# Output layers of three attentions as three products of rounded parts, and the second block's norms moved behind the products

## The chip, the core and the metric

The kernel runs on one core of one Trainium2 chip. The metric is device time in microseconds (us), the median of three runs. The profiler's record of one execution gives the rows below.

## The reference, cut to what matters

Two blocks follow each other on x, 512 tokens by 1024 features, all in fp32. The first has two layers; each is FFN, mixer, FFN, and the mixers are a pair of attentions (FoX and a top-k "DSA") in layer 0 and MLA in layer 1:

```
h = h + 0.5*g1*swiglu(rms(h)*(1+sc1)+sh1)
h = h + g2*mixer(rms(h)*(1+sc2)+sh2)      # mixer ends in: mixed @ w_out
h = h + 0.5*g3*swiglu(rms(h)*(1+sc3)+sh3)
h = rmsnorm(h, final_g)                   # end of the first block
```

The second block has two layers more: `u = rmsnorm(h, norm1)`, an input layer for three mixers (mLSTM, differential attention, HGRN), `h += mixed @ w_out`, then `h += relu(rmsnorm(h, norm2) @ w_up)**2 @ w_down`. A norm divides each token (a column of h) by the root of its mean square.

## The kernel before, in words

Features lie on the partitions: h, u are 8 chunks of 128 features by 512 tokens. A dense layer goes slab by slab: a slab holds the weights for 256 outputs (2048 columns; for a down layer 128 outputs), SP loads it into one of four slots of `ring`, and waits for `lin_done` of the slab four before. `ORDER` lists all layers; its last field says whether a layer is *cut*.

In a cut layer weights and inputs are each split into a rounded part (fp32r) and a remainder, and each pair of 128x128 weights and 128x512 inputs is three products: high x high, remainder x high, high x remainder. ScalarE writes a slab's rounded part (`high(q)`, into one of two halves of `w_hi`, after `lin_done` of cut slab q-2), GpSimd the remainder in place in the ring (`rest(q)`, then `w_cut`). Both run two slabs ahead (`layer`). The uncut layers multiply whole fp32. These are `mlaq`, `mlak`, `mlav` and the output layers `hybo`, `mlao`, `wo0`, `wo1`; the last four have 4 slabs of 16 pairs each.

A norm before a layer: ScalarE squares each chunk when it is final (`hrms`), GpSimd adds the squares up (`squares`), PE sums over partitions (`total_sum`), ScalarE takes the root, VectorE the reciprocal, PE spreads it over the partitions (`spread`), VectorE scales each chunk into u (`scale_in`), ScalarE rounds it (`high_input`), VectorE takes the remainder. In `linear`, slab 0 of such a layer takes its products in the order in which chunks arrive (`Fresh`). With `cut_at` (4, 6) the first two slabs of the next layer are rounded ahead of chunks 4 and 6 of the squares, with (7,) one ahead of chunk 7 and the other after.

The attentions go in steps of one head (or two) and 128 queries: PE scores, VectorE maximum, ScalarE exp, VectorE scaling of E (L1828, L1874), PE transposes, ScalarE copy, PE values. ScalarE and VectorE each work through one fixed order, written out by hand. After the last head, `hybo` or `mlao` reads u. In the second block the mLSTM's 16 steps stand between the differential attention and `wo`; `out_products` does chunks 2 to 7 of `wo` slabs 0 and 1 while the mLSTM's own norm (chunks 0, 1) is under way.

## Time and profile before

| | |
|---|---|
| median of 3 runs | 3743.09 us (3741.81 to 3745.54) |
| the profiled execution: time | 3749.99 us |
| its span | 3748.2 us |
| mean granted TensorE clock | 0.963 |
| PE busy | 96% of the span |
| VectorE, ScalarE, GpSimd busy | 37%, 26%, 40% |

The span is shorter than the time by what lies ahead of the first and behind the last instruction. PE is TensorE's matrix products, PEld its weight loads, DVE VectorE, ACT ScalarE, POOL GpSimd, SP the engine that issues DMAs. A row's first numbers are the start and the length in us from the span's start, or, in groups, a busy time and a mean. The arrow behind a name gives what ended the idle time before the instruction.

### The profile page before, as it was taken

Reading aid. Unit: us, or ns where it says so; the run is one execution under the profiler, and the core shown is the slowest. Engines: PE = TensorE matmul, PEld = TensorE weight load, DVE = VectorE, ACT = ScalarE, POOL = GpSimd, SP = SyncE. Lnnn points to the kernel's source line nnn. Section 1 sums busy time; section 2 is a strip of 40 time slices with the busy share of each in tenths; the row PEclk is TensorE's granted clock in tenths of the full one; section 3 lists DMA queues with packets and bytes.
Section 4 is the critical chain, followed back from the end, with each engine's and each line's share of the span. In section 5 each row is a group of like instructions: output and inputs, shape, how many; then the busy total and the mean of one; then the engine's idle time right before and its main releaser. Section 6 shows DMA issues by size and latency. Waiting matters only on the chain.

```text
span 3748.2 us, 41071 instructions
## 1 busy us (share of the span) xinstructions
PE 3597.0 (96%) x16200; PEld 2740.0 (73%) x16200; DVE 1385.3 (37%) x2572; ACT 965.4 (26%) x1205; POOL 1490.6 (40%) x521
## 2 busy tenths in 40 slices
PE   8999999799999999999999989989999999799999
PEld 7878777558887888755688866843888869437887
DVE  4454277624243422233210145752201267632010
ACT  2222222522223212303222233331212233312221
POOL 3445451025454545400354554401546445014453
PEclk9999998899999999999999989988999999799999
DMA  6434221025343433220223222101222212002222
GB/s 247 184 140 177 98 79 57 1 79 191 119 190 114 189 123 136 81 99 12 79 80 105 88 76 79 68 1 45 90 91 100 90 68 79 12 34 79 101 90 79
DMA packets 53863, 360.58 MB, mean 96 GB/s; under 512 B 5968, under 2 KB 6352, under 8 KB 16592
## 3 DMA queue, kind: packets, MB, share of 16 engines
q1 hardware_dynamic: 53712, 358.53, 26.4%
q8 instruction: 100, 1.64, 0.2%
q14 instruction: 51, 0.42, 0.0%
HBM read 356.41 MB, written 2.10 MB: 96 GB/s over the span
## 4 chain that ended last, share of the span: by engine, by line
PE 90%; DVE 6%; ACT 1%; issue 1%; DMA 1%; POOL 1%; SPq 0%; DVEq 0%; ACTq 0%; POOLq 0%
PE LP L459 80%; PE XB L459 9%; DVE S L1814 1%; PE LP L747 1%; DMA big<-w_ada 1%; PE XB L631 0%; ACT E L1060 0%; DVE tmp L1936 0%; DVE st L1934 0%; POOL wk L1481 0%; ACT sq L1060 0%; DVE wk L1834 0%; DVE gain L1651 0%; DVE stat L1826 0%; POOL w_lo L1423 0%
## 5 line engine op out<-in xcount | busy, mean ns | idle before, releaser
L1423 POOL TENSOR_TENSOR w_lo<-ring,w_hi 128x2048 fp32r<-128x2048 f32 (+1 forms) x263 | 1122.9, 4270 | 682.8 <-ACT w_hi L1060 682.0
L459 PE MATMUL LP<-u_hi,w_hi 128*128 128x512 f32 x2480 | 992.9, 400 | 21.2 <-ACT u_hi L1060 17.0
L459 PE MATMUL LP<-u_hi,w_lo 128*128 128x512 f32 x2480 | 980.5, 395 | 0.0
L459 PE MATMUL LP<-u_lo,w_hi 128*128 128x512 f32 x2480 | 937.6, 390 | 0.0
L459 PE MATMUL LP<-big_r,w_hi 128*128 128x512 f32 x2432 | 749.6, 389 | 1.2 <-POOL w_lo L1423 1.2
L1060 ACT ACTIVATE w_hi<-ring 128x2048 fp32r<-128x2048 f32 (+1 forms) x263 | 468.7, 1782 | 813.9 <-PE LP L459 726.1
L459 PEld LDWEIGHTS LP<-u_hi,w_hi 128*128 128x128 f32 x2480 | 475.5, 192 | 137.3 <-issue 39.1
L459 PEld LDWEIGHTS LP<-u_hi,w_lo 128*128 128x128 f32 x2480 | 474.9, 192 | 102.2
L459 PEld LDWEIGHTS LP<-u_lo,w_hi 128*128 128x128 f32 x2480 | 467.0, 188 | 95.2 <-issue 0.5
L459 PEld LDWEIGHTS LP<-big_r,w_hi 128*128 128x128 f32 x2432 | 455.9, 188 | 95.6 <-issue 1.3
L459 PE MATMUL LP<-big_r,w_lo 128*128 128x512 f32 x1216 | 473.2, 389 | 0.0
L1464 POOL TENSOR_TENSOR big_r<-tmp,big_r 128x512 f32 (+2 forms) x120 | 192.5, 1604 | 687.6 <-DVE big_r L1667 687.6
L1481 POOL TENSOR_TENSOR wk<-wk,sq 128x512 f32<-128x512 f32 x66 | 84.7, 1284 | 697.2 <-ACT sq L1060 694.2
L1060 ACT ACTIVATE tmp<-LP 128x512 f32<-128x512 f32 (+1 forms) x121 | 86.1, 711 | 971.1 <-PE LP L459 971.1
L1672 DVE TENSOR_TENSOR tmp<-tmp,LP 128x512 f32<-128x512 f32 x88 | 60.6, 688 | 635.1 <-ACT tmp L1060 620.7
L459 PEld LDWEIGHTS LP<-big_r,w_lo 128*128 128x128 f32 x1216 | 228.3, 188 | 47.7
L459 PE MATMUL LP<-u,ring 128*128 128x512 f32 x512 | 224.7, 600 | 4.2 <-DVE u L2284 2.6
L1580 DVE SCALAR_TENSOR_TENSOR XB<-ada_in,csil,XB 128x256 f32<-128x256 f32 x390 | 191.1, 490 | 13.7
L459 PEld LDWEIGHTS LP<-u,ring 128*128 128x128 f32 x512 | 97.7, 192 | 128.8 <-issue 122.6
L1742 DVE SCALAR_TENSOR_TENSOR h<-LP,gate,h 128x512 f32 (+1 forms) x64 | 48.1, 751 | 357.0 <-PE LP L459 356.5
L1060 ACT ACTIVATE E<-S,stat 128x128 f32<-128x128 f32 (+3 forms) x160 | 89.2, 558 | 241.4 <-DVE stat L1817 161.8
L2296 DVE TENSOR_TENSOR tmp<-tmp,LP 128x1024 f32<-128x1024 f32 x32 | 39.1, 1222 | 280.9 <-ACT tmp L1060 280.9
(266 smaller groups left out, 3259.8 us busy)
## 6 DMA issues: line engine op xcount, KB each, us to landing
ada_in<-w_ada SPq DMA_DIRECT2D x66, 1024.0 KB, 4.9
ring<-w_in SPq DMA_DIRECT2D x22, 1024.0 KB, 4.8
ring<-w_gu00a SPq DMA_DIRECT2D x11, 1024.0 KB, 7.1
ring<-w_gu00b SPq DMA_DIRECT2D x11, 1024.0 KB, 6.6
ring<-w_gu01a SPq DMA_DIRECT2D x11, 1024.0 KB, 6.8
ring<-w_gu01b SPq DMA_DIRECT2D x11, 1024.0 KB, 6.7
ring<-w_gu10a SPq DMA_DIRECT2D x11, 1024.0 KB, 6.7
ring<-w_gu10b SPq DMA_DIRECT2D x11, 1024.0 KB, 7.0
```

The costliest lines, as they stand in the source:

```text
L459: return pe.matmul(o, lhsT=lhsT, rhs=rhs, start=start, stop=stop)
L747: last = pe.transpose(LP[1][:, j, blk(b)], E[:, 2 * (k % 2) + j, blk(b)], cc("ident"))
L1060: return act.activation(o, i, fn, **kw)
L1423: gp.tensor_tensor(w_lo[:, slab % RING, 0:width], ring[:, slab % RING, 0:width], w_hi[:, q % 2, 0:width].bitcast(F32), ALU.subtract).then_ ...
L1464: gp.tensor_tensor(big_r[:, lo, :], src, big_r[:, hi, :].bitcast(F32), ALU.subtract)\
L1481: gp.tensor_tensor(sqa, sqa, sq[:, c % 2, :], ALU.add).then_inc(s("sq_added"), 1)
L1580: ins = stt(part if c < DC - 1 else ada_acc[:, :], wv[:, c * 256:(c + 1) * 256], csil[:, c:c + 1], part, ALU.mult, ALU.add)
L1672: tt(o, tmp[:, p, 0:T].unsqueeze(1), LP[p][:, 1:2, :], ALU.mult))
L1742: stt(o, LP[p][:, 0:1, :], g, o, ALU.mult, ALU.add).then_inc(s(f"lin_taken{p}"), 1)
L1814: link(dve.tensor_tensor_reduce(out=S[:, k % 2, 0:W], in0=XB[k % 2][:, 0:W], in1=mask(qb, W), scale=1.0, scalar=LOWEST, op0=ALU.add, op1=A ...
L2296: cut_hidden(k, it, p, pl.low, 2, lambda o: tt(o, o, LP[p][:, :, :], ALU.mult))
```

## The change

All four output layers become cut layers. The rounded weights of their slabs go to parts of `big` that the attention no longer needs (`w_high`), two homes in turn. The outputs of finished heads are rounded by ScalarE in the attention's steps (`cut_output`, `high_mixed`), and their remainders taken by GpSimd (`rest_mixed`); the first two slabs are cut beside the attention too. In `wo` each pair becomes three products, and the order changes a little.

In the second block, the four norms go behind the products. ScalarE rounds h times the gain, unnormalised (`late_chunk`), VectorE takes the remainder (`late_input`), PE multiplies, and in slab 0 sums the squares between the high and the low products (`total_sum(late)`), and spreads the root's reciprocal after the slab (`spread(late)`). It is kept as R, and every result is multiplied by it when it is taken from PSUM. In front of the first of them the final norm of the first block is folded in: two sums (of h squared and of h times final_g squared), two spreads, and h is scaled beside slab 1. Squares of these chunks start beside the last down layer (`final_chunk`, `final_square`). relu and square change places: VectorE takes relu times R from PSUM, ScalarE squares. The layers `up0a` and `up1a` are written out instead of looped. The diff, cut to its core and moved left:

```diff
-ORDER += [("hyb", 10, DC * 256, 0, 1), ("hybv", 4, DC * 256, 0, 1), ("hybo", 4, DC * 256, 0, 0)]
+ORDER += [("hyb", 10, DC * 256, 0, 1), ("hybv", 4, DC * 256, 0, 1), ("hybo", 4, DC * 256, 0, 1)]
...
-          ("mlav", 4, 2 * 256, 0, 0), ("mlao", 4, DC * 256, 0, 0)]
+          ("mlav", 4, 2 * 256, 0, 0), ("mlao", 4, DC * 256, 0, 1)]
...
-    ORDER += [(f"in{l}", 11, DC * 256, 0, 1), (f"inv{l}", 4, DC * 256, 0, 1), (f"wo{l}", 4, DC * 256, 0, 0)]
+    ORDER += [(f"in{l}", 11, DC * 256, 0, 1), (f"inv{l}", 4, DC * 256, 0, 1), (f"wo{l}", 4, DC * 256, 0, 1)]
...
+CUT_SLABS, HIGH_HOME, slabs = [], [], 0
+HIGH_CHUNKS = {"hybo": (FK, FV), "mlao": (0, KN), "wo0": (AQ, AK), "wo1": (AQ, AK)}
...
+def w_high(q, width):
+    if HIGH_HOME[q]:
+        c = HIGH_HOME[q][0]
+        return big_r[:, c:c + 4, :].rearrange("p a b -> p (a b)")[:, 0:width]
+    return w_hi[:, q % 2, 0:width]
...
+def mixed_high(name, c):
+    if name == "hybo":
+        return big_r[:, FQ + c if c < 4 else DQ + c - 4, :]
+    return big_r[:, QN + c if name == "mlao" else AV + c, :]
...
-    return 4 if pl.slab == 0 else n_ada if 0 < n_ada < n else None
+    return 4 if pl.slab == 0 or name in ("up0a", "up1a") else n_ada if 0 < n_ada < n else None
...
-                high, rest = w_hi[:, (pl.cut + k) % 2, 0:width], w_lo[:, slot, 0:width]
+                high, rest = w_high(pl.cut + k, width), w_lo[:, slot, 0:width]
...
                         mm(LP[p][:, f, :], rest[:, cols(c, f)], fresh.high[:, c, :], start=False, stop=False)
+                if fresh.late:
+                    total_sum(fresh.late)
...
+            if k == 0 and fresh is not None and fresh.late:
+                spread(fresh.late)
...
-    def total_sum():
+    def total_sum(late=0):
...
+        for i in range(2 if late == 2 else 1):
+            pl.got("seconds_summed" if i else "squares_summed")
+            for b in range(NB):
+                mm(XB[1][:, 4 * i + b:4 * i + b + 1], square_home(0, late, i)[:, blk(b)], cc("ones", 0, 1),
+                   start=b == 0 and i == 0, stop=False)
+        for i in range(2 if late == 2 else 1):
+            pl.got("seconds" if i else "h_squared", DC)
+            for b in range(NB):
+                last = mm(XB[1][:, 4 * i + b:4 * i + b + 1], square_home(DC - 1, late, i)[:, blk(b)],
+                          cc("ones", 0, 1), start=False, stop=b == NB - 1 and i == (late == 2))
...
-    def spread():
+    def spread(late=0):
         pe.wait_ge(s("rstd_ready"), pl.norm)
+        if late == 2:
+            for b in range(NB):
+                mm(XB[3][:, blk(b)], first4[:, b:b + 1].to_broadcast([P, P]), cc("ident"))
...
+    def mixed(name):
+        ready = set()
+        def src(c):
+            if c not in ready:
+                ready.add(c)
+                pl.got("mix_cut")
+            return mixed_high(name, c), u_lo[:, c, :]
+        return src
...
-    linear("hybo", "fm", lambda c: u[:, c, :])
+    linear("hybo", "fm", mixed("hybo"))
...
-    total_sum()
-    spread()
     for l in range(DEPTH):
-        src, fresh = norm(u_hi2)
+        src, fresh = late_norm(twice=l == 0)
...
+        src = mixed(f"wo{l}")
...
             slab, group = pl.slab + k, pl.group + k
             slot, p = slab % RING, group % 2
+            high, rest = w_high(pl.cut + k, DC * 256), w_lo[:, slot, :]
             if chunks[0] == 2:
                 pe.wait_ge(s(f"lin_taken{p}"), group // 2)
-                pe.wait_ge(s(f"w_in{slot}"), 16 * (slab // RING + 1))
+                pe.wait_ge(s("w_cut"), pl.cut + k + 1)
             for c in chunks:
+                u_high, u_rest = src(c)
                 for f in range(2):
-                    last = mm(LP[p][:, f, :], ring[:, slot, c * 256 + f * P:c * 256 + f * P + P], u[:, c, :],
-                              start=c == 2, stop=c == 1)
+                    o, cols = LP[p][:, f, :], slice(c * 256 + f * P, c * 256 + f * P + P)
+                    mm(o, high[:, cols], u_high, start=c == 2, stop=False)
+                    mm(o, rest[:, cols], u_high, start=False, stop=False)
+                    last = mm(o, high[:, cols], u_rest, start=False, stop=c == 1)
             if chunks[-1] == 1:
                 last.then_inc(s("lin_done"), 1)
...
-        out_products(1, range(2, DC))
+        out_products(1, range(2, 6))
         pl.got("num_recip")
         for cp in range(2):
             last = mm(XB[2 + cp][:, :], cc("sel4", cp * P, P)[0:4, :], mix_rows[0:4, :])
         last.then_inc(s("num_spread"), 1)
-        pl.got("mix_ready")
+        out_products(1, range(6, DC))
...
-        src, fresh = norm(u_hi2)
+        src, fresh = late_norm()
...
-        f(w_hi[:, q % 2, 0:width], ring[:, slot, 0:width], ACT.Copy).then_inc(s("w_high"), 1)
+        f(w_high(q, width), ring[:, slot, 0:width], ACT.Copy).then_inc(s("w_high"), 1)
+    def high_mixed(name, c, n=1):
+        o = mixed_high(name, c)
+        if n == 1:
+            f(o, u[:, c, :], ACT.Copy).then_inc(s("mix_high"), 1)
+        else:
+            f(big_r[:, AV + c:AV + c + n, :], u[:, c:c + n, :], ACT.Copy).then_inc(s("mix_high"), n)
...
+    def late_chunk(c, gains, twice):
+        f(u_hi2[:, c, :], h[:, c, :], ACT.Copy, scale=gains[:, c:c + 1]).then_inc(s("u_high"), 1)
+        if c >= 3:
+            act.wait_ge(s("sq_added"), pl.seen.get("sq_added", 0) + c - 2)
+        f(square_home(c, True), h[:, c, :], ACT.Square).then_inc(s("h_squared"), 1)
+        if twice:
+            if c >= 3:
+                act.wait_ge(s("second_added"), c - 2)
+            f(square_home(c, True, True), h[:, c, :], ACT.Square, scale=sp_("final_g", c)).then_inc(s("seconds"), 1)
+    def final_chunk(k):
+        if k < DC - 2:
+            g = pl.group + k
+            act.wait_ge(s(f"lin_taken{g % 2}"), g // 2 + 1)
+            if k == 0:
+                act.wait_ge(s("total_ready"), pl.seen.get("total_ready", 0))
+                pl.got("gain_ready")
+            late_chunk(k, gain, True)
...
+    def late_rms(gains, per=1, cut_at=(7,), twice=False):
+        act.wait_ge(s("total_ready"), pl.seen.get("total_ready", 0))
+        for c in range(DC - 2 if twice else 0, DC):
+            for j, chunk in enumerate(cut_at):
+                if chunk == c:
+                    high(pl.cut + j)
+            pl.chunk_final(c, per)
+            late_chunk(c, gains, twice)
+        pl.passed("sq_added", DC - 2)
+        for q in range(len(cut_at), 2):
+            high(pl.cut + q)
+        pl.got("total_ready")
+        if pl.norm:
+            act.wait_ge(s("rstd_ready"), pl.norm)
+        f(rt4, XB[1][:, 0:NB], ACT.Sqrt, scale=1.0 / D, bias=cc("eps")).then_inc(s("rt_ready"), 1)
+        pl.norm += 1
+        if twice:
+            pl.got("second_mean")
+            f(mean4, mean4, ACT.Sqrt, bias=cc("eps")).then_inc(s("second_root"), 1)
...
+            layer(down + part, angles if up + part == "gu00a" else None, last=part == "b",
+                  behind=final_chunk if down + part == "dn11b" else None)
...
+    def cut_output(name, c):
+        pl.got("o_taken")
+        high_mixed(name, c)
+    def behind_fox(n):
+        if n in (7, 11, 15):
+            cut_output("hybo", n // 4 - 1)
+    def behind_dsa(n):
+        if n == 1:
+            cut_output("hybo", 3)
+        if n in (3, 5):
+            high(pl.cut + (n - 3) // 2)
+        if n in (7, 11, 15):
+            cut_output("hybo", n // 4 + 3)
+    duo_attention(FOX_H // 2, lambda n: take_gates(4 + n, [LP[0][:, 1, :]]) if n < 4 else None, behind_fox)
+    duo_attention(DSA_H // 2, behind=behind_dsa)
+    cut_output("hybo", 7)
+    layer("hybo", last=True)
...
-    attention(MLA_H, 192.0 ** -0.5, P)
-    skip("mlao")
+    def beside_heads(n):
+        if n % NB == 3 and NB < n < 8 * NB:
+            cut_output("mlao", n // NB - 1)
+        if n in (9, 21):
+            high(pl.cut + n // 21)
+    attention(MLA_H, 192.0 ** -0.5, P, beside=beside_heads)
+    cut_output("mlao", 7)
+    layer("mlao", last=True)
...
-    hrms()
-    pl.tu += DC
     for l in range(DEPTH):
-        if l:
-            hrms()
-        else:
-            hrms(cut_at=(), normed=True)
-        high(pl.cut + 1)
-        high_input(u_hi2)
+        late_rms(sp_("norm1", l * DC, DC) if l else gain, twice=l == 0)
...
+            if n in (3, 4):
+                high(pl.cut + n - 3)
+            if 10 <= n < 16:
+                act.wait_ge(s("mix_scaled"), 6 * l + n - 9)
+                if n >= 14:
+                    pl.got("h_gated")
+                high_mixed(f"wo{l}", n - 8)
...
-        skip(f"wo{l}")
-        hrms(2, (4, 6))
-        high_input(u_hi2)
+        pl.got("mix_ready")
+        high_mixed(f"wo{l}", 0, 2)
+        layer(f"wo{l}", last=True)
+        late_rms(sp_("norm2", l * DC, DC), 2, (4, 6))
...
+            def square(k, it):
                 p = (g0 + k) % 2
-                f(tmp[:, p, :], LPF[p], ACT.Relu).then_inc(s("silu_done"), 1)
-            layer(f"up{l}{part}", relu)
+                act.wait_ge(s(f"lin_taken{p}"), at((g0 + k) // 2 + 1, it, RING // 2))
+                f(tmp[:, p, :], tmp[:, p, :], ACT.Square).then_inc(s("silu_done"), 1)
...
-                         w_hi[:, q % 2, 0:width].bitcast(F32), ALU.subtract).then_inc(s("w_cut"), 1)
+                         w_high(q, width).bitcast(F32), ALU.subtract).then_inc(s("w_cut"), 1)
+    def rest_mixed(name, *chunks):
+        for c in chunks:
+            pl.got("mix_high")
+            gp.tensor_tensor(u_lo[:, c, :], u[:, c, :], mixed_high(name, c).bitcast(F32), ALU.subtract)\
+                .then_inc(s("mix_cut"), 1)
...
+    def late_squares(cut_at=(7,), twice=False):
+        for c in range(DC - 2 if twice else 1, DC):
+            if c == DC - 1:
+                gp.nop().then_inc(s("squares_summed"), 1)
+                if twice:
+                    gp.nop().then_inc(s("seconds_summed"), 1)
+            for j, chunk in enumerate(cut_at):
+                if chunk == c:
+                    rest(pl.cut + j)
+            if c == DC - 1:
+                break
+            late_square(c, twice)
+        pl.passed("h_squared", DC)
+        for q in range(len(cut_at), 2):
+            rest(pl.cut + q)
...
+    def final_square(k):
+        if 1 <= k < DC - 2:
+            late_square(k, True)
...
-    skip("hybo")
+    rest_mixed("hybo", 0, 1, 2, 3)
+    rest(pl.cut)
+    rest(pl.cut + 1)
+    rest_mixed("hybo", 4, 5, 6, 7)
+    layer("hybo", last=True)
...
+    rest_mixed("mlao", 0)
+    rest(pl.cut)
+    rest_mixed("mlao", 1, 2, 3)
+    rest(pl.cut + 1)
+    rest_mixed("mlao", 4, 5, 6, 7)
+    layer("mlao", last=True)
...
-        skip(f"wo{l}")
-        first_input((4, 6))
+        rest(pl.cut)
+        rest(pl.cut + 1)
+        rest_mixed(f"wo{l}", 2, 3, 4, 5, 6, 7)
+        pl.passed("mix_high", 2)
+        layer(f"wo{l}", last=True)
+        late_squares((4, 6))
...
+    def late_input(gains, twice=False):
+        for c in range(DC):
+            pl.got("u_high")
+            stt(u_lo[:, c, :], h[:, c, :], gains[:, c:c + 1], u_hi2[:, c, :].bitcast(F32), ALU.mult, ALU.subtract)\
+                .then_inc(s("u_ready"), 1)
+        dve.wait_ge(s("rt_ready"), pl.norm + 1)
+        pl.norm += 1
+        if twice:
+            link(dve.reciprocal(first4, rt4))
+            link(tt(mean4, first4, first4, ALU.mult))
+            stt(mean4, XB[1][:, NB:2 * NB], 1.0 / D, mean4, ALU.mult, ALU.mult).then_inc(s("second_mean"), 1)
+            pl.got("second_root")
+            link(dve.reciprocal(mean4, mean4))
+            tt(root4(0, NB), mean4, first4, ALU.mult).then_inc(s("rstd_ready"), 1)
+        else:
+            dve.reciprocal(root4(0, NB), rt4).then_inc(s("rstd_ready"), 1)
+        pl.got("rstd_spread")
+        link(dve.tensor_copy(R, XB[0][:, :]))
...
-    scale_in(h, sp_("final_g", 0, DC))
-    dve.wait_ge(s("u_scaled"), pl.tu)
     for l in range(DEPTH):
         init = 0.8 - 0.6 * math.exp(-0.3 * l)
-        scale_in(u, sp_("norm1", l * DC, DC), u_hi2)
+        late_input(sp_("norm1", l * DC, DC) if l else gain, twice=l == 0)
...
+            pl.got("qk_summed")
+            link(tt(qk_rows(i), XB[0][0:8, :], R[0:8, :], ALU.mult))
+            tt(qk_rows(i), qk_rows(i), R[0:8, :], ALU.mult).then_inc(s("qk_means"), 1)
             pl.got("qk_root")
-            dve.reciprocal(qk_rows(i), qk_rows(i)).then_inc(s("qk_recip"), 1)
+            link(dve.reciprocal(qk_rows(i), qk_rows(i)))
+            tt(qk_rows(i), qk_rows(i), R[0:8, :], ALU.mult).then_inc(s("qk_recip"), 1)
...
-            ts(big[:, c:c + 2, :], LP[p][:, :, :], scale, None, ALU.mult).then_inc(s(f"lin_taken{p}"), 1)
+                ts(big[:, c:c + 2, :], LP[p][:, :, :], sp_("qn" if k < 3 else "kn", l), None, ALU.mult)\
+                    .then_inc(s(f"lin_taken{p}"), 1)
+            else:
+                tt(big[:, c:c + 2, :], LP[p][:, :, :], over_two(R), ALU.mult).then_inc(s(f"lin_taken{p}"), 1)
             if k == 0:
                 gates_begin()
+                for i in range(DC) if l == 0 else ():
+                    stt(h[:, i, :], h[:, i, :], sp_("final_g", i), XB[3][:, :], ALU.mult, ALU.mult)
...
-            values(k, it, p)
+            tt(values[k], LPF[p].rearrange("p (t c) -> p t c", c=256), per_token, ALU.mult)\
+                .then_inc(s(f"lin_taken{p}"), 1)
...
         tt(u[:, 0:2, :], u[:, 0:2, :], XBS[:, 2:4, :], ALU.mult).then_inc(s("mix_ready"), 1)
+        dve.wait_ge(s("mix_high"), 16 + 8 * (l + 1))
+        tt(u_lo[:, 0:2, :], u[:, 0:2, :], big_r[:, AV:AV + 2, :].bitcast(F32), ALU.subtract)\
+            .then_inc(s("mix_cut"), 2)
...
-        scale_in(u, sp_("norm2", l * DC, DC), u_hi2)
+        late_input(sp_("norm2", l * DC, DC))
...
+            if pl.low + k >= 2:
+                dve.wait_ge(s("h_cut"), at(pl.low + k - 1, it, RING))
+            o = tmp[:, p, :].rearrange("p (a b) -> p a b", a=2)
+            stt(o, LP[p][:, :, :], 0.0, over_two(R), ALU.max, ALU.mult).then_inc(s(f"lin_taken{p}"), 1)
             dve.wait_ge(s("silu_done"), at(pl.silu + k + 1, it, RING))
-            cut_hidden(k, it, p, pl.low, 2, lambda o: tt(o, o, LP[p][:, :, :], ALU.mult))
+            ts(big_r[:, dyn(big, k, it, 2, 2), :], o, 1.0, None, ALU.mult).then_inc(s("h_high"), 1)
```

## Rows read from the trace of the kernel before

**Rows 1.** The page, busy time of each engine: us, share of the span, instructions
```profile
PE 3597.0 (96%) x16200; PEld 2740.0 (73%) x16200; DVE 1385.3 (37%) x2572; ACT 965.4 (26%) x1205; POOL 1490.6 (40%) x521
```
**Rows 2.** The page, chain that ended last, shares by line
```profile
PE LP L459 80%; PE XB L459 9%; DVE S L1814 1%; PE LP L747 1%; DMA big<-w_ada 1%; PE XB L631 0%; ACT E L1060 0%; DVE tmp L1936 0%; DVE st L1934 0%; POOL wk L1481 0%; ACT sq L1060 0%; DVE wk L1834 0%; DVE gain L1651 0%; DVE stat L1826 0%; POOL w_lo L1423 0%
```
**Rows 3.** The chain in order of time: a gu01 slab; hybo whole
```profile
1034.97 11.05 PE LP L459 x48
...
746.56 55.22 PE LP L459 x128
```
**Rows 4.** The chain in order of time: end of the first block, start of in0
```profile
2179.89 5.68 PE LP L459 x25
...
2188.84 1.17 PE XB L459 x8
...
2208.21 30.28 PE LP L459 x120
```
**Rows 5.** The chain in order of time: wo0 and the start of up0a
```profile
2547.66 10.50 PE LP L459 x24
2558.15 1.81 PE XB L459 x4
...
2573.68 37.44 PE LP L459 x80
...
2622.44 17.70 PE LP L459 x67
```
**Rows 6.** The chain in order of time: wo1 and the start of up1a
```profile
3319.17 10.50 PE LP L459 x24
...
3373.79 6.02 PE LP L459 x14
...
3383.34 2.10 PE XB L459 x16
...
3389.66 16.43 PE LP L459 x60
```
**Rows 7.** The chain in order of time: end of down0b, start of in1
```profile
2969.93 3.19 PE LP L459 x14
...
2980.18 15.98 PE LP L459 x58
```
**Rows 8.** Timeline at the end of the first block: cutting, squares, rounding, differences
```profile
2182.77 1.90 ACT L1060 ACTIVATE w_hi<-ring 128x2048 fp32r<-128x2048 f32 x1
2183.01 1.31 POOL L1481 TENSOR_TENSOR wk<-wk,sq 128x512 f32<-128x512 f32 x1 [0.86 <-ACT sq L1060]
...
2184.75 4.52 POOL L1423 TENSOR_TENSOR w_lo<-ring,w_hi 128x2048 fp32r<-128x2048 f32 x1 [0.43 <-ACT w_hi L1060]
...
2207.44 5.24 ACT L1060 ACTIVATE u_hi<-u 128x512 fp32r<-128x512 f32 x8 [1.43 <-DVE u L1630]
...
2211.93 4.91 DVE L1636 TENSOR_TENSOR u_lo<-u,u_hi 128x512 fp32r<-128x512 f32 x8
```
**Rows 9.** The chain in order of time: the sums of gu01a's norm
```profile
805.50 3.56 PE XB L459 x16
```
**Rows 10.** Timeline, DVE, between wo0's slabs 0 and 1
```profile
2561.97 3.34 DVE L2282 RECIPROCAL ada_in<-ada_in 4x512 f32<-4x512 f32 x1
```
**Rows 11.** Timelines of DVE and POOL in hyb and in0: overlapping instructions
```profile
502.43 5.07 POOL L1423 TENSOR_TENSOR w_lo<-ring,w_hi 128x2048 fp32r<-128x2048 f32 x1
503.67 4.39 DVE L1791 TENSOR_TENSOR big<-big 128x512 f32<-128x512 f32 x1
...
2297.20 4.62 POOL L1423 TENSOR_TENSOR w_lo<-ring,w_hi 128x2048 fp32r<-128x2048 f32 x1 [7.81 <-ACT w_hi L1060]
2300.63 1.93 DVE L2107 TENSOR_SCALAR big<-big,st 128x512 f32<-128x512 f32 x2 [3.66 <-ACT big L1060]
2302.49 0.87 DVE L2111 TENSOR_SCALAR big<-big,st 128x512 f32<-128x512 f32 x2
```
**Rows 12.** Stretches: length, busy times, PE clock (DSA attention; MLA attention)
```profile
680.00:746.00 66.00, 53.66 (x412) 34.36 (x410) 35.33 (x135) 36.22 (x97) 0.00 (x0) 0.86 0.00 1
...
1680.00:1758.00 78.00, 73.80 (x363) 43.74 (x362) 39.86 (x165) 30.69 (x96) 0.00 (x0) 1.00 0.06 26
```

88 lines of the change are left out of this document (50 added, 38 removed).

## The prediction

> **What bounds the kernel now.** The page's busy times come first: PE is busy for 96% of the span [rows 1], so anything that helps must shorten PE's own work or the few stretches in which PE waits. The chain that ended last agrees: 80% of it is PE writing LP, the products of the dense layers [rows 2]. Next I read that chain in order of time, because it shows both what one slab costs and where PE stops. A cut slab (16 pairs of weights and input, three products each, 48 records) takes 11.05 us; the uncut output layer of the hybrid attention has 64 pairs, shows 128 records, two for each pair, and takes 55.22 us [rows 3]. So a pair costs 55.22/64 = 0.863 us whole and 3 x 11.05/48 = 0.69 us as three products of rounded parts. The DMA queues are on the chain only at the start; I leave them out, since the same slabs are loaded at the same points (a cut slab's DMA waits for the same count as before).
>
> The rest of PE's loss lies at norms. Before the second block's first layer, the last product of the first block ends at 2185.57 and slab 0 ends at 2208.21 + (30.28 - 72 x 0.228) = 2222.1: 36.5 us for a slab that takes 11 [rows 4]. At the other norms of the second block the same measure, from the last product to the end of the next slab 0, is 24.7 us (2611.12 to 2635.8) [rows 5], 23.4 us [rows 6] and 20.8 us [rows 7]. Part of it is the clock: the first slab takes about 13.7 us instead of 11.
>
> **The output products.** *hybo and mlao*: 64 x (0.863 - 0.69) = 11.05 us less each. The cutting is beside the attention, and the last output chunk needs 0.65 us on ScalarE (5.24 for eight roundings of a chunk) and 1.3 on GpSimd [rows 8] while PE is still at chunks 0 to 6 of slab 0: hidden. Slabs 2 and 3: ScalarE's rounding of a slab takes 1.90 us and GpSimd's remainder 4.52 [rows 8], and both wait for the end of the slab two before, so 6.5 us against a slab of 11: hidden.
>
> But the same wait is now written for the slabs behind. `high(q)` waits for `lin_done` of slab q-2 of the cut ones. For the second slab of gu01 or gu11 that slab was long past; now it is the last slab of the output layer. In `hrms` and `squares` this rounding and its remainder stand ahead of chunk 6. GpSimd's last addition of squares therefore comes 0.1 + 1.90 + 4.52 + 1.3 = 7.8 us after the last product; before, PE's sums began 3.7 us after it (801.78 to 805.50) [rows 3, 9]. That gives back 4.2 us at both places, and at mlao about 1 us more, since a longer idle PE finds itself at the lower clock (the sums' 16 records take 3.56 us there, and 2.10 at full clock [rows 6, 9]).
>
> *wo0 and wo1.* Before: 2547.66 to 2611.12 = 63.5 us, and 3319.17 to 3379.81 = 60.6 us [rows 5, 6]. After, from PE's start t: 36 records for chunks 2 to 7 of slab 0, 8.2; the sum of squares 1.9 (1.81 in [rows 5]; t+10.1); 24 records 5.5 (t+15.6), while VectorE comes through steps of one and two chunks (0.65 each, 2.0) and the reciprocal, 3.34 [rows 10], just in time; the spread 1.9 (t+17.5); VectorE's product of two chunks 1.2 (2 x 0.61), ScalarE's copy of them 1.0 (half of 1.90), VectorE's difference 1.2 (t+21.1 with the starts), while PE does 12 records and waits 1 us; then 12 records end slab 0 at t+23.9 and 12 end slab 1 at t+26.7. Slab 2's rounding waits for the end of slab 0: 23.9 + 0.1 + 1.90 + 4.52 = t+30.5. PE stands still for 3.8 us and comes back at the lower clock: a slab of 13.7 (t+44.2), then 11.0 (t+55.2). So -8 and -5; as the 1 us wait may drop the clock too, I take -7 and -4.5.
>
> **The norms.** *norm2, both layers.* h is rounded and fed to PE unnormalised, so PE goes on at once: 32 high records 7.3 us, behind which the sum waits for GpSimd until 7.8 (the same second-slab wait as above), 2.1, then 16 low records 3.65 and the spread 1.1 [rows 4]: 14.7 us to the end of slab 0 against 24.7 and 23.4. VectorE's eight differences (0.61 each, 4.91 for eight [rows 8]) start after 1.3 us; even held up until GpSimd is free they are done at 13, before PE needs the last. So -10 and -8.7. *First norm, second layer*: the second rounding is behind chunk 7, nothing waits: 7.3 + 2.1 + 3.65 + 1.1 = 14.2 against 20.8, -6.6. *First norm of the block*: GpSimd adds the two sums of chunk 6 (2 x 1.3), then takes slab 0's remainder (4.52): from the end of the last but one slab (7.5 us earlier) 0.8 + 1.3 + 2 x 1.3 + 4.52 = 9.3, so PE waits 1.8 us; then 7.3, four groups of sums 4.2, 3.65, two spreads 2.3: 19.3 against 36.5, -17; with an even chance of a drop of the clock (2.7), -16. The eight scalings of h (0.65 each) go to VectorE beside slab 1, which has 11 us.
>
> **What is added elsewhere.** ScalarE gets in each of the first two attentions 8 copies (0.65) and 2 roundings (1.90), and GpSimd 8 differences (1.3) and 2 remainders (4.52). GpSimd was idle there, and that matters. A VectorE `tensor_tensor` with both inputs in SBUF takes 0.61 us alone (the differences of [rows 8]) and 4.39 under a remainder of 5.07; a `tensor_scalar` inside SBUF takes 1.93 for two instead of 0.87 when it starts under one [rows 11]. The attentions scale E with just such an instruction in every step. The Trainium skill (SBUF - State Buffer, "Who interferes with whom") says the same as a rule: a VectorE instruction with two SBUF inputs, or a `tensor_scalar` in its two-port mode, and a GpSimd one shut each other out for a whole instruction. By that rule the trace agrees, and it speaks against placing this work here.
>
> Prices: VectorE blocked for some 3 us by each remainder, of which a step's slack hides a part: VectorE is idle 38 of 78 us over some 30 steps in the MLA attention, 1.3 a step, and 31 of 66 us over 16 in the DSA attention, 1.9 [rows 12]. I take 2 us exposed each; the small differences fit into the slack. In the DSA attention ScalarE is on the chain too (busy 36.2 of 66 us, PE 53.7 [rows 12]): its roundings expose 1 us each, its copies 0.3. Sum 4 + 2 + 1 = 7 us for hybo. In the MLA attention PE is busy 73.8 of 78 [rows 12]: 5 us. In the mLSTM stretch the two remainders fall into PE's own sums: 1 us a layer. Bounds: nothing, if all is in the slack; and above, each of 2 x (4.52 + 1.90) + 8 x 0.65 exposed, 18 us for each of the first two, and 6 for each mLSTM stretch, 48 in all.
>
> The rest costs nothing: relu and square trade places within a slab of 11 us in which ScalarE and VectorE wait for PE; the two more products and the later reciprocal at `qk_recip` (2 us more of VectorE twice a layer) fit into the half slab before PE asks for the spread; without that cover they cost 4 us a layer. The unrolled up layers change no time of a product.
>
> **Sum**, against the profiled execution (span 3748.2, time 3750.0, that is 6.9 above the median 3743.1): hybo -11.05 + 4.2 + 7 = 0; mlao -11.05 + 5.2 + 5 = -1; wo0 and wo1 -11.5, mLSTM +2; norms -10 - 8.7 - 6.6 - 16 = -41.3. Together -52: a median of 3743 - 52 = 3691 us.
>
> **Rivals.** (A) *The attentions absorb the cutting.* For it: GpSimd idle, ScalarE under 55% busy; against it: the locked instructions of [rows 11]. Then -52 - 14 = -66: 3677. Chance 0.24. (B) *The waits cost more*: about 35 of the 48 us are exposed: -66 + 35 = -31: 3712. Chance 0.16. (C) *Slower*: GpSimd's remainders hold up VectorE, and PE behind it, in every attention and also in the in-layers, where `qk_recip` now has an instruction with two SBUF inputs four times in the block, each up to 4.5 (18 us). It decides from 66 us exposed, which is all of 48 + 18, and gives 3743, or 3751 if three more waits drop the clock at 2.7 each. Chance 0.03. (D) *The change does not do what it says at the norms*: PE keeps stopping, as the first product waits for w_cut of slab 0 or the sum for GpSimd; then only a third of the 41 us comes: -52 + 27 = -25: 3718. Against it: slab 0's rounding needs only the slab before last. Chance 0.07. The forecast itself: 0.50.
>
> The likeliest is 3691. The range goes from A's 3677 with some margin for shorter waits, 3672, to between B and D, 3713. A change of 0.2% (7.5 us) is about what three runs can tell. Faster 0.95, same 0.02, slower 0.03.
>
> **What would show it.** The hybo stretch of chain should read about 44 us for 192 records, then sums that begin near 8 us after it. wo0 should show a stop of almost 4 us before its third slab. No gap of more than 2 us before in0, and slab 0 of up0a without a wait at its start. The `E` scalings of VectorE (0.44 us for 512 columns in [rows 11]) should show single ones of 3 to 5 us under GpSimd's remainders, and the two attentions should be 7 and 5 us longer. If their length is unchanged, A holds; if hybo's records are not at 0.23 us, or the clock stays low through a whole slab after a stop, the prediction is wrong.

## The result, and the profile after

The changed kernel takes 3714.14 us (median of 4 runs, 3712.59 to 3720.33) where the kernel before took 3744.32 in the same set of runs: 0.9919 of it, interval 0.9903 to 0.9934. So it is faster, by 30 us, where 52 were forecast; 3691 was said, and a range that ends at 3713. A second set of five rounds of the same kernel (e_same, below) gave 3712.9 and 0.9900 (0.9885 to 0.9916). The experiments below ran in three later sets, each beside the kernel before, whose median there was 3749.4 to 3750.5 us; so kernels of different sets are better compared by their ratios to it than by their times.

The profiled executions differ by 36.2 us of span (3748.2 to 3712.0), since the one of before (3749.99 us) lay 5.7 us above its median and the one of the changed kernel (3714.21) at its own. The page of the changed kernel, busy times and the lines of the chain that answer to [rows 1] and [rows 2]:

```profile
PE 3559.4 (96%) x16456; PEld 2786.8 (75%) x16456; DVE 1418.3 (38%) x2562; ACT 1011.1 (27%) x1246; POOL 1601.8 (43%) x565
PE LP L483 79%; PE XB L483 9%; POOL w_lo L1561 1%; DVE S L2031 1%; DMA big<-w_ada 1%; PE LP L802 1%; PE XB L686 1%; ACT E L1119 0%; DVE tmp L2153 0%; DVE st L2151 0%; ACT w_hi L1119 0%; DVE wk L2051 0%; DVE gain L1867 0%; DVE stat L2043 0%; ACT sq L1119 0%
```

The kinds of work are the same, but GpSimd's remainders (w_lo) now stand on the chain for about 1% of the span. Where, the chain in order of time says (start, length, what), from hybo to the end of slab 0 of the second block:

```profile
748.59 43.87 PE LP L483 x192
794.88 4.50 POOL w_lo L1561
800.79 3.56 PE XB L483 x16
808.74 13.54 PE LP L483 x48
...
1698.13 4.25 issue
1733.19 4.25 issue
1765.87 43.83 PE LP L483 x192
1811.83 4.50 POOL w_lo L1561
1817.74 3.56 PE XB L483 x16
...
2185.49 4.56 POOL w_lo L1561
2190.29 7.54 PE LP L483 x32
2197.83 3.46 PE XB L483 x32
2201.29 3.74 PE LP L483 x16
2206.82 16.36 PE LP L483 x72
```

hybo takes 43.87 us for its 55.22 in [rows 3], at 0.228 us a record. Behind it, the remainder of the next layer's second slab (794.88) now stands between the last product and the sum of squares: the norm takes 16.3 us for 11.7. The two "issue" pieces of 4.25 us inside the MLA attention are new; nothing like them stands in the chain of before. And the 36.5 us at the border of the blocks [rows 4] have shrunk. The same view of the second block:

```profile
2429.60 4.56 PE LP L483 x56
2542.05 8.40 PE LP L483 x36
2568.74 4.54 POOL w_lo L1561
2573.42 24.45 PE LP L483 x96
2600.01 4.90 POOL w_lo L1561
2604.91 1.68 POOL rstd L1617
2606.77 1.92 PE XB L483 x16
2608.69 5.37 PE LP L483 x16
2614.95 10.91 PE LP L483 x48
...
2966.20 16.36 PE LP L483 x72
...
3189.64 4.56 PE LP L483 x56
3294.25 8.43 PE LP L483 x36
3351.87 4.90 POOL w_lo L1561
3366.80 10.91 PE LP L483 x48
```

Here PE stops once in wo0, before its third slab, for 4.0 us (from 2569.4 to 2573.42, behind the remainder at 2568.74), where 3.8 was forecast; a second remainder (2600.01) stands in front of norm2's sum. Stage by stage, with the terms of the prediction's sum beside what the two chains give ("mLSTM" is the stretch from the 56-record piece at 2429.60 to the start of wo0, 2445.67 to 2547.66 before):

| stage | forecast | measured | us before, after |
|---|---|---|---|
| FoX and DSA attention | +7 | +3.5 | 164.2, 167.7 |
| hybo | -11.05 | -11.35 | 55.22, 43.87 |
| norm behind it | +4.2 | +4.6 | 11.7, 16.3 |
| MLA attention | +5 | **+11.6** | 79.7, 91.3 |
| mlao | -11.05 | -11.4 | 55.22, 43.83 |
| norm behind it | +5.2 | +5.3 | 10.7, 16.0 |
| norm between the blocks | -16 | -16.9 | 398.0, 381.1 with the FFN before it |
| mLSTM, layer 0 | +1 | **+10.5** | 102.0, 112.5 |
| wo0 | -7 | -7.6 | 63.5, 55.8 |
| norm2, layer 0 | -10 | **-7.6** | 24.7, 17.1 |
| first norm, layer 1 | -6.6 | -6.9 | |
| mLSTM, layer 1 | +1 | +2.8 | 101.8, 104.6 |
| wo1 | -4.5 | -5.1 | 60.6, 55.5 |
| norm2, layer 1 | -8.7 | **-6.4** | 23.4, 17.1 |
| all the rest | 0 | -1.3 | |
| sum | -51.5 | -36.2 | |

Eight terms are within 1 us. The loss is in the MLA attention, in the mLSTM (of layer 0 above all), and in the two norm2. The first can be seen directly. Timeline of the changed kernel, start, length and instruction (what ended an idle time stands in brackets):

```profile
1697.80 4.66 DVE L2045 TENSOR_SCALAR E<-E,stat 128x256 f32<-128x256 f32 x1
1697.81 4.50 POOL L1561 TENSOR_TENSOR w_lo<-ring,big_r 128x2048 fp32r<-128x2048 f32 x1 [3.62 <-ACT big_r L1119]
...
1702.61 0.41 PE L686 MATMUL XB<-cst,E 128*128 128x128 f32 x2 [2.64 <-DVE E L2045]
```

A scaling of E that lasts 0.4 us otherwise lasts 4.66, as long as GpSimd's remainder beside it, and PE waits for it. Over the whole attention VectorE's 32 scalings of E take 21.0 us here and 12.4 where nothing is cut there (e_norms): 8.6 us more for two remainders.

### The profile page after: what moved, and what is told of

It is laid out like the page before. It is cut to its first block, busy times and chain, and to the rows that moved or that the text cites. A ratio compares the mean times of both kernels' runs of the same rounds, so it can differ in the third digit from the quotient of the medians.

```text
span 3712.0 us, 41467 instructions
## 1 busy us (share of the span) xinstructions
PE 3559.4 (96%) x16456; PEld 2786.8 (75%) x16456; DVE 1418.3 (38%) x2562; ACT 1011.1 (27%) x1246; POOL 1601.8 (43%) x565
## 4 chain that ended last, share of the span: by engine, by line
PE 89%; DVE 6%; issue 1%; ACT 1%; POOL 1%; DMA 1%; SPq 0%; DVEq 0%; ACTq 0%; POOLq 0%
PE LP L483 79%; PE XB L483 9%; POOL w_lo L1561 1%; DVE S L2031 1%; DMA big<-w_ada 1%; PE LP L802 1%; PE XB L686 1%; ACT E L1119 0%; DVE tmp L2153 0%; DVE st L2151 0%; ACT w_hi L1119 0%; DVE wk L2051 0%; DVE gain L1867 0%; DVE stat L2043 0%; ACT sq L1119 0%
## 5 line engine op out<-in xcount | busy, mean ns | idle before, releaser
L483 PE MATMUL LP<-big_r,w_lo 128*128 128x512 f32 x1472 | 575.1, 391 | 0.0
L483 PEld LDWEIGHTS LP<-big_r,w_lo 128*128 128x128 f32 x1472 | 277.7, 189 | 57.6
L1119 ACT ACTIVATE tmp<-LP 128x512 f32<-128x512 f32 x89 | 53.2, 598 | 707.6 <-PE LP L483 707.6
L1561 POOL TENSOR_TENSOR w_lo<-ring,big_r 128x2048 fp32r<-128x2048 f32 x16 | 72.6, 4542 | 260.3 <-ACT big_r L1119 260.3
L1568 POOL TENSOR_TENSOR u_lo<-u,big_r 128x512 fp32r<-128x512 f32 x28 | 35.8, 1282 | 275.7 <-ACT big_r L1119 275.7
L2533 DVE TENSOR_TENSOR h<-h,LP 128x512 f32 x32 | 22.0, 687 | 317.0 <-PE LP L483 317.0
L483 PE MATMUL XB<-big 64*128 64x128 f32 (+5 forms) x472 | 127.4, 508 | 16.1 <-DVE stat L2034 6.1
```

Source lines behind the costliest of these rows:

```text
L483: return pe.matmul(o, lhsT=lhsT, rhs=rhs, start=start, stop=stop)
L1119: return act.activation(o, i, fn, **kw)
L1561: gp.tensor_tensor(w_lo[:, slab % RING, 0:width], ring[:, slab % RING, 0:width], w_high(q, width).bitcast(F32), ALU.subtract).then_inc(s(" ...
L1568: gp.tensor_tensor(u_lo[:, c, :], u[:, c, :], mixed_high(name, c).bitcast(F32), ALU.subtract)\
L2533: tt(o, o, LP[p][:, 0:1, :], ALU.add).then_inc(s(f"lin_taken{p}"), 1)
```

## The experiments

Theory L: a VectorE instruction that meets a GpSimd remainder waits for all of it, and each remainder of 2048 columns beside an attention costs its 4.5 us whole; the other losses are the `lin_done` waits of the rounding. Its rival R: the attentions are longer because ScalarE and GpSimd have more to do in all, whatever the pieces. A third, the clock rival (the rival R of the expectations of e_split and e_norms): TensorE's granted clock fell, in the mLSTM above all, for a reason that has nothing to do with the cutting. Where an expectation gives some 70 us for the mLSTM, it counts from a later start; the lengths measured here are those of the table's stretch.

### The first two remainders in four pieces: e_split

```diff
+def rest_in_four(q):
+    slab, width = CUT_SLABS[q]
+    gp.wait_ge(s("w_high"), q + 1)
+    for i in range(4):
+        c = slice(i * T, i * T + T)
+        ins = gp.tensor_tensor(w_lo[:, slab % RING, c], ring[:, slab % RING, c],
+                               w_high(q, width)[:, c].bitcast(F32), ALU.subtract)
+    ins.then_inc(s("w_cut"), 1)
...
-            rest(pl.cut)
+            rest_in_four(pl.cut)
-            rest(pl.cut + 1)
+            rest_in_four(pl.cut + 1)
```

> Edit: the remainders of the first two slabs of each output layer, which GpSimd takes beside the attention, are four instructions of 512 columns (about 1.3 us each) instead of one of 2048 (4.50 us). Theory L (locks): in the changed kernel's MLA attention the chain shows two stops of 4.25 us, each under one such remainder, while a scaling of E took 4.66 us instead of 0.35. With pieces VectorE is shut out for at most one piece: the MLA attention shortens from 91 us by 6 to 9, the DSA attention by 1 to 3, total 7 to 12 us less than the changed kernel, 3702 to 3707. Rival R (only the clock): VectorE stays shut out while one piece follows the other, or the time lies in TensorE's lower clock (0.92 in the MLA attention after, 1.00 before), which the pieces do not touch: no change, within 3 us.

Measured: 3699.58 us, 0.9876 (0.9860 to 0.9892), somewhat better than L said. The MLA attention is back at 79.9 us, the FoX and DSA attention at 164.9 (that this second gain is not firm, e_all_s1 and e_all_s3 show below). The same place in its timeline:

```profile
1693.57 1.43 DVE L2055 TENSOR_SCALAR E<-E,stat 128x256 f32<-128x256 f32 x1
1693.57 5.12 POOL L1570 TENSOR_TENSOR w_lo<-ring,big_r 128x512 fp32r<-128x512 f32 x4 [3.61 <-ACT big_r L1119]
...
1696.76 0.80 DVE L2055 TENSOR_SCALAR E<-E,stat 128x384 f32<-128x384 f32 x1
```

GpSimd takes slightly longer in all (5.12 us for 4.50), and VectorE gets in between the pieces: 1.43 us in place of 4.66. The same work in the same place then costs the MLA attention almost nothing, so R is out: the length of the piece was the cost. The clock rival is out for this stage too: the attention's granted clock is 1.00 with the pieces and 0.93 with the whole remainders, so the lower clock came with the stops.

### The second slab's wait taken away: e_free

```diff
-                if q >= 2:
+                if q >= 2 and not (HIGH_HOME[q - 2] and not HIGH_HOME[q]):
                     act.wait_ge(s("lin_done"), at(CUT_SLABS[q - 2][0] + 1, it, RING))
```

The slab two before had a place of its own, which this one doesn't overwrite, so nothing has to be waited for.

> Edit: the rounding of a slab waits no more for the slab two before where that one had a home of its own (the four slabs of an output layer), so the first two slabs of the next layer can be rounded during the output layer. Theory: this wait is what moved the norm behind hybo from 11.7 to 16.3 us and behind mlao from 10.7 to 16.0, and holds up the sum in slab 0 of both up layers (a wait of 1.7 us and 1.9 us in the sum and low products). Expected 4.5 + 5.0 + 2 x 2 = 13 us less than the changed kernel, 3701, with the norms back at 11 to 12. Rival: GpSimd is the bound there anyway (its two remainders and six additions are 17 us in the last two slabs of 22), and the norm shortens by less than 2 us each: 3710.

Measured: 3697.47 us, 0.9861 (0.9846 to 0.9876). Its chain behind hybo:

```profile
750.17 43.83 PE LP L483 x192
794.02 1.42 DVE h L1984 x2
796.26 1.27 POOL wk L1656
797.72 3.09 PE XB L483 x16
805.20 12.68 PE LP L483 x48
```

That is better than the 3701 expected, and far from the rival's 3710. No w_lo stands between product and sum; the norms take 11.2 and 11.1 us for 16.3 and 16.0, and wo with norm2 68.6 in each layer for 72.9 and 72.6. The MLA attention keeps its 91.8 us: the two losses are separate.

### The norms alone: e_norms

All four output layers whole again, the second block's norms behind the products. The core:

```diff
-("hybo", 4, DC * 256, 0, 1)
+("hybo", 4, DC * 256, 0, 0)
...
-    linear("hybo", "fm", mixed("hybo"))
+    linear("hybo", "fm", lambda c: u[:, c, :])
```

> Edit: only the norms part of the change; the four output layers are whole fp32 again, with nothing cut beside the attentions. Theory L: the norms keep their gain (17 before in0, 7 before in1, about 10 before each up layer, 43 in all) and the attentions and both mLSTM stretches are as long as before the change: 3700, that is less than the changed kernel, so that the output part as written costs more than it gives. The mLSTM stretch of the first layer, from the last attention output to wo0, is back from 72 to 62 us. Rival R (clock): the 9.7 us in that stretch come from a lower TensorE clock (0.63 for its last 32 us) that the cutting has nothing to do with; then it stays about 70 us, and the kernel is at 3710.

Measured: 3716.39 us, 0.9914 (0.9899 to 0.9928), the same as the changed kernel. So the output layers' half of the change brings next to nothing as it was made: what it saves in products it gives back in the attentions and behind them. But 3716 is 16 us above what L expected, and the missing time is in the mLSTM stretches, in which this kernel cuts nothing:

```profile
2422.18 4.56 PE LP L483 x56
2532.99 10.50 PE LP L483 x24
...
3182.99 4.56 PE LP L483 x56
3293.43 10.50 PE LP L483 x24
```

110.8 and 110.4 us for 102.0 and 101.8 in the kernel before. Cutting beside them is not what made them long: this kernel has the same 319 products, 166 instructions of VectorE and 86 of ScalarE there as the kernel before. This is what the recorded rival (the clock, with 3710 us) had said, and theory L's forecast of a short stretch failed.

### Four places for the rounded slabs of wo: e_homes

```diff
-"wo0": (AQ, AK), "wo1": (AQ, AK)}
+"wo0": (AQ, AK, HQ, XQ), "wo1": (AQ, AK, HQ, XQ)}
...
                 f(Z[:, 0:2, :], XBS[:, 0:2, :], ACT.Square).then_inc(s("num_squared"), 1)
+                high(pl.cut + 2)
+                high(pl.cut + 3)
```

It has e_free's edit too.

> Edit: as the freed wait, and in addition the four slabs of wo0 and wo1 have four homes, and slabs 2 and 3 are rounded right after the squares of the mLSTM's numerator, so that none of them waits for a slab of wo. Theory: wo0 and wo1 lose the stop before their third slab (4.5 us on the chain under GpSimd's remainder) and the half-speed start behind it (2.7): 55.5 to about 48.5 us each. Together with the freed wait 13 + 14 = 27 us less than the changed kernel: 3687. Rival: the remainders of slabs 2 and 3 (9 us of GpSimd) now lie beside VectorE's steps with two SBUF inputs in the mLSTM's norm and lock one of them, so that the norm becomes late by up to 4.5 us: 3692 to 3696.

Measured: 3693.08 us, 0.9842 (0.9829 to 0.9856): faster than e_free, but within the rival's figures and 6 us above the theory's. wo with its norm takes 62.7 and 63.1 us, and its chain through norm2 has no stop:

```profile
2586.27 1.68 PE XB L484 x16
2587.95 3.74 PE LP L484 x16
...
2592.59 10.91 PE LP L484 x48
```

With its norm, wo is some 10 us shorter in each layer than in the changed kernel; wo0 itself takes 49 us (48.5 expected), and PE waits 0.85 us for the mLSTM's norm in its slab 0 as in the changed kernel. So the rival's late norm is not there, though its time is met. The 6 us missing lie in its second mLSTM stretch: 115.1 us where e_free has 107.7. Its five executions fall into two groups, 3684.8 and 3685.9 against 3693.1 to 3693.9, and the profiled one (3693.38) is of the second. Two of the five were thus faster than the theory's 3687, and the gap between the groups, some 8 us, is about what the long stretch costs; that the fast two have a short stretch is not shown, as neither was profiled.

### mlao alone whole again: e_mlao_whole

```diff
-("mlao", 4, DC * 256, 0, 1)
+("mlao", 4, DC * 256, 0, 0)
...
-            attention(MLA_H, 192.0 ** -0.5, P, beside=beside_heads)
-            cut_output("mlao", 7)
-            layer("mlao", last=True)
+            attention(MLA_H, 192.0 ** -0.5, P)
+            skip("mlao")
```

> The changed kernel with mlao alone not cut: its slabs as 32 fp32 products each again, nothing rounded or subtracted beside the MLA attention; everything else stays. If the ledger is right, the MLA attention is 11.6 us shorter (79.7 for 91.3), the norm behind mlao 5.3 us shorter (10.7 for 16.0) and the four slabs 11.4 us longer (55.2 for 43.8): 5.5 us faster than the changed kernel, 3708.6. Cutting mlao was then a loss. Rival, with the prediction's own sizes (attention 5, norm 5.2, slabs 11.05): 0.85 us slower than the changed kernel, 3715. A second rival, that the longer attention is owed to something other than the cutting of mlao: the attention stays near 91 us, and the time is about 3720.

Measured: 3709.0 us, 0.9893 (0.9878 to 0.9908), beside 3712.9 of the changed kernel in the same set. The intervals overlap, so the whole alone does not settle it; the stages are as expected one by one: attention 79.7 us, four slabs 55.2, norm 11.0, in sum some 5 us less than in the changed kernel. Cutting mlao was a small loss as it was made.

### The changed kernel again, and both repairs: e_same and e_all

> The changed kernel itself, unchanged, beside the three others of this set. It measures what a second profile of the same program differs by. If the granted clock of the mLSTM stretches is a matter of the moment, at least one of the two stretches (from the 56 low-rank products to the start of wo0 or wo1: 112.5 and 104.6 us in the first profile, 102.0 and 101.8 in the kernel before) comes out 3 us or more away from its first length, with the same instructions. If the cutting beside them sets it, both come back within 1 us. Its time in either case: 3714, give or take 4.

> Both repairs together: the remainders of the first two slabs of the four output layers as four pieces each (as in e_split), and four places for the rounded slabs of wo0 and wo1, with none of the waits for the products of two slabs before (as in e_homes). By the ledger of the two: e_homes' 3693.1, less the 3 us of the FoX and DSA attentions and the 11.8 us of the MLA attention that the pieces took away in e_split; the norms behind hybo and mlao are short already. That is 3678, with a few us either way for the clock of the mLSTM stretches. The MLA attention (from the first product of its denominators to the start of mlao) should take 80 us as in e_split, not 91.8 as in e_homes. Rival: the two repairs remove the same idle time, or the granted clock takes the gain; then it is 3687 to 3693.

Measured: e_same 3712.9 us (3712.59 to 3714.15); e_all 3673.12 us, 0.9795 (0.9782 to 0.9808), 40 us faster than the changed kernel beside it. That is 5 us better than the 3678 expected: the repairs add up. Attentions 164.8 and 81.2, norms 11.6 and 11.7, wo with norm2 62.6 twice. In e_same the mLSTM stretches took 108.1 and 107.7 where the first profile of the same program had 112.5 and 104.6. The stages in all these kernels, us:

| stage | before | after | e_same | e_split | e_free | e_norms | e_homes | e_all |
|---|---|---|---|---|---|---|---|---|
| FoX, DSA | 164.2 | 167.7 | 167.7 | 164.9 | 167.4 | 162.0 | 167.7 | 164.8 |
| behind hybo | 11.7 | 16.3 | 16.3 | 16.3 | 11.2 | 11.7 | 11.1 | 11.6 |
| MLA | 79.7 | 91.3 | 90.5 | 79.9 | 91.8 | 79.7 | 91.8 | 81.2 |
| behind mlao | 10.7 | 16.0 | 16.0 | 16.0 | 11.1 | 10.7 | 11.1 | 11.7 |
| mLSTM 0 | 102.0 | 112.5 | 108.1 | 107.9 | 107.9 | 110.8 | 108.0 | 108.1 |
| mLSTM 1 | 101.8 | 104.6 | 107.7 | 107.7 | 107.7 | 110.4 | 115.1 | 107.8 |
| wo0, norm2 | 88.2 | 72.9 | 72.1 | 72.1 | 68.6 | 75.7 | 62.7 | 62.6 |
| wo1, norm2 | 84.0 | 72.6 | 72.1 | 72.1 | 68.6 | 75.9 | 63.1 | 62.6 |

### Moving the mLSTM in time: e_shifted, e_shifted1, e_all_s1, e_all_s3

One copy of VectorE in the differential attention, some 20 us ahead of the stretch (in e_shifted1 0.68 us long, at 2421.0), is repeated. e_shifted and e_shifted1 do it in the kernel before, with four repeats and one, e_all_s1 and e_all_s3 in e_all, with one and three. The edit with four:

```diff
-                            ins = dve.tensor_copy(o, i)
+                            for _ in range(4 * cp):
+                                link(dve.tensor_copy(o, i))
+                            ins = dve.tensor_copy(o, i)
```

> The kernel before, with nothing of the change in it; in the differential attention of both layers, some 30 us ahead of the mLSTM's decay products, VectorE repeats one copy of 128x512 four times (some 0.7 us each) and so moves all that follows. If the mLSTM stretch was short in the kernel before (102.0 and 101.8 us) because its pauses happened to fall well for the clock, one of the two stretches becomes 3 us or more longer than the shift itself, and the whole is 6 to 20 us above the kernel before. If the changed kernels' own instructions there make it long, both stretches stay at 102 us but for the shift, and the whole is 3 to 6 us above the kernel before.

> The kernel before with one repeated copy in each differential attention instead of e_shifted's four (0.7 us for 2.8). In e_shifted the two mLSTM stretches took 115.0 and 111.0 us for 102.0 and 101.8 in the kernel before, with the same instructions. If any small change of timing ahead of them costs the short state, one stretch at least is 3 us or more above 102 here as well, and the whole 5 to 20 us above the kernel before. If only the longer pause of TensorE brings the lower clock, both stretches stay at 102, and the whole is about 1.4 us above the kernel before.

> e_all with one repeated copy (0.7 us) in each differential attention, ahead of the mLSTM stretches, which took 108.1 and 107.8 us in e_all. If their length is a matter of how their pauses fall in time, it moves: 3 us or more up or down in one of them, and the whole leaves 3671 to 3677. If the changed kernels' instructions fix it, both stay within 1 us of 108, and the whole is 1.4 us above e_all, 3674.5.

> The same with three copies (2.1 us). By timing: at least one stretch moves by 3 us or more against e_all or e_all_s1; if one of the two kernels reaches the 102 us of the kernel before in both layers, it is the fastest yet, about 3665. By the instructions: both stretches at 108, the whole 4.2 us above e_all, 3677.3.

Measured: e_shifted 3770.66 us; its ten executions fall into two groups, four at 3748.5 to 3750.7 and six at 3770.5 to 3774.7, so its ratio, 1.0023 (0.9997 to 1.0048), says little. e_shifted1 3761.45 us, 1.0036 (1.0025 to 1.0047): one more copy of 0.7 us in each of two layers, and 11 us lost; its ten executions (3759.3 to 3764.5) all lie above the thirteen of the kernel before beside it (3741.6 to 3758.1). e_all_s1 3675.14 us, 0.9806 (0.9784 to 0.9828), and e_all_s3 3676.18 us, 0.9806 (0.9785 to 0.9828). The windows of the stretches, with the same 319 products in each: span, its length, busy PE, PEld, DVE, ACT and POOL, then the granted clock (1.00 is 2.4 GHz), DMA share and GB/s. Kernel before:

```profile
2445.67:2547.66 101.99, 89.41 (x319) 37.26 (x319) 54.45 (x166) 34.34 (x86) 0.00 (x0) 0.83 0.00 1
3217.36:3319.17 101.81, 89.77 (x319) 37.18 (x319) 54.43 (x166) 34.35 (x86) 0.00 (x0) 0.83 0.00 1
```

e_shifted1, with nothing of the change:

```profile
2440.01:2550.28 110.27, 98.93 (x319) 39.39 (x319) 54.43 (x166) 34.35 (x86) 0.00 (x0) 0.75 0.00 1
3218.28:3328.56 110.28, 99.04 (x319) 39.44 (x319) 54.42 (x166) 34.36 (x86) 0.00 (x0) 0.75 0.00 1
```

The changed kernel, first profile:

```profile
2429.60:2542.05 112.45, 100.84 (x319) 41.02 (x319) 57.76 (x166) 40.85 (x94) 16.55 (x8) 0.73 0.00 1
3189.64:3294.25 104.61, 92.39 (x319) 38.35 (x319) 58.58 (x166) 40.85 (x94) 16.56 (x8) 0.80 0.00 1
```

The changed kernel, second profile (e_same):

```profile
2430.91:2538.97 108.06, 97.18 (x319) 40.45 (x319) 57.89 (x166) 40.85 (x94) 16.54 (x8) 0.76 0.00 1
3185.64:3293.32 107.68, 95.73 (x319) 39.57 (x319) 57.88 (x166) 40.86 (x94) 16.53 (x8) 0.78 0.00 1
```

Length goes with clock, from 102 us at 0.83 to 112.5 at 0.73 (e_shifted has 115.0 at 0.72), and VectorE's and ScalarE's busy time don't move between the first two pairs. In the twelve profiles other than that of before, 24 stretches, none is at 102: they lie between 104.6 and 115.1. So the one profile of the kernel before shows a short state of these two stretches which no other profile has, not even of the same instructions moved by 0.7 us.

A profile shows one execution, though, and two things limit this. The four faster executions of e_shifted, which were not profiled, lie 22 us below the six slower ones, and 22.2 us is what its two stretches (115.0 and 111.0) are above 102.0 and 101.8: an estimate from these numbers is that the faster four had the short state, so a shift does not always lose it. And e_all_s1 (109.6 and 107.5) and e_all_s3 (107.1 and 107.9) moved little: one of the four stretches by more than 1 us, none by 3. There the expectation of a large move was a miss, and the other one, that the changed kernels' instructions fix the length near 108, gave the times nearly (3674.5 and 3677.3 for 3675.14 and 3676.18). Thirteen of the twenty stretches of the changed kernels lie between 107.5 and 108.1. Whether a kernel with the change can reach 102 at all is open.

The last two runs show one thing more. Up to hybo their instructions are those of e_all, and their FoX and DSA attention took 168.0 and 169.4 us, at a granted clock of 0.84, where e_all and e_split have 164.8 and 164.9 at 0.88, all four with the remainders in pieces. With whole remainders five profiles lie between 167.3 and 167.7; with nothing cut there, it is 162.0, 162.0 and 160.6 (e_norms, e_shifted1, e_shifted), and 164.2 in the profile of before. So in this attention a gain by the pieces is not shown. In the MLA attention it is: 79.9, 81.2, 79.9 and 79.9 us with pieces, 90.5 to 91.8 without.

## Why the prediction was wrong

The direction and most of the mechanism were right; the forecast is 23 us too low, and the range missed by 1. By the two chains, 15 of the 23 are in the terms of the sum: 6.6 in the MLA attention, 11.3 in the mLSTM and 4.7 in the two norm2, less 3.5 in the FoX and DSA attention and some 4 in all the others. The rest, some 7 us, is the base. Point by point:

**Right.** The price of a pair (-11.35 and -11.4 for -11.05), the wait of the second slab behind hybo and mlao (+4.6 and +5.3 for +4.2 and +5.2), the stop in wo and its size (4.0 for 3.8 us), the sign of all four norm terms, and two of them to 1 us: the first norm of layer 1 (-6.9 for -6.6) and the norm between the blocks (-16.9 for -16), where PE waits for the remainder of slab 0:

```profile
2190.29 0.47 PE L483 MATMUL LP<-u_hi,w_hi 128*128 128x512 f32 x1 [2.68 <-POOL w_lo L1561]
```

e_free and e_homes show the two waits to be those named: taken away, their times go.

**The MLA attention, +5.** The step that failed is "VectorE blocked for some 3 us by each remainder, of which a step's slack hides a part", 2 us exposed each. The right rows had been read [rows 11], but the price was set below them on the ground of mean idle time (VectorE 38 of 78 us idle [rows 12]). The chain runs through the locked instruction, and the slack of 1.3 us a step hid nothing of either lock: each stands on the chain with its whole 4.25 us. Measured: 8.6 us more in E's scalings, two of 4.25 on the chain, and a further 3 us while the granted clock was 0.93 over the attention, where it was 1.00 without the locks. With the remainders in pieces it is +0.3 in three profiles and +1.6 in e_all. Two sums there do not follow from their parts either: two remainders at 2 us make 4 and not 5, and 4 + 2 + 1 = 7 has 1 us for copies priced at 0.3. The Trainium skill (SBUF - State Buffer, "Who interferes with whom") says that whoever issues first has the shared ports for the whole instruction and the other fully blocks. The trace agrees on the length: the scaling ended at 1702.46, 0.15 us behind the remainder's end at 1702.31. On who issued first it says nothing firm, since the two start at 1697.80 and 1697.81. The rule suggests the repair too, since what counts is the length of one instruction.

**The mLSTM, +1 a layer.** The sum took the stretches of before as fixed and asked what the cutting would add. The cutting adds little that can be told apart (108 us in e_all and 110 to 111 in e_norms, which cuts nothing there); what changed is the granted clock, with PE 97 to 99% busy in the second half. VectorE was busy 57.9 us a stretch with whole remainders (e_same) and 54.6 with pieces (e_split), and the length stayed at 108: the locks cost nothing here. +10.5 and +2.8 in the first profile, +6.1 and +5.9 in the second, and +8.3 and +8.5 in the kernel before with a copy more. This is the second step that failed, and the larger one: the prediction took the clock of these stretches as given and had no term for it; it allowed for single drops of 2.7 us, behind waits. Why the clock is lower in the changed kernels stays open.

**norm2, -10 and -8.7.** The step is "even held up until GpSimd is free they are done at 13, before PE needs the last". The remainder took 4.90 us for 4.52 and the addition behind it 1.68 for 1.3, so the sum began 8.9 us after the last product and not 7.8; and the eight differences, 4.91 us alone, took 10.75 around the lock, so that the 16 low products needed 5.4 us for 3.65. Measured -7.6 and -6.4. In e_homes, where the remainder is long done, the low products take 3.74.

**The FoX and DSA attention, +7.** Against the profile of before it cost 3.5 us. But that profile is long in this stage (164.2 us): the five profiles with whole remainders are 5.3 to 7.1 us above the three others without cutting. So the term was nearly right, and it looks too large only against this base.

**The base.** The prediction took its rows from an execution 6.9 us above the median and subtracted the whole sum from the median. The two profiles differ by 36.2 us, the medians by 30.2: 6 us are what this one execution of the kernel before was slow by. The traces show where. With the same instructions e_shifted1 and e_shifted reach hybo at 740.47 and 740.24 us, this execution at 746.56. (The median of before had also moved, from 3743.1 to 3744.3.)

**The rivals.** B named the time, 3712, but by luck: it wanted 35 of 48 us of cutting exposed. What was exposed is 12 us in the MLA attention and 3.5 to 7 in the FoX and DSA attention; the rest of the way is the clock of the mLSTM, norm2 and the base (whose 7 us no rival had). A fell (no attention absorbed whole remainders), C and D fell too: the stretch from slab 1 of in0 to the mLSTM took 222.8 us for 223.6, and PE went from wo0 into up0a without a pause. One sign was missed by a little: no stop of over 2 us was to stand before in0, and it is 2.68.

How much of the mLSTM's loss is the position in time, and how much the changed kernels' own instructions, is not settled. Why 0.7 us moves the granted clock of such a stretch by 0.08, and why e_shifted runs at two times, stays open; no run here looked into what the clock follows.
